# The opening product of each feature-major FFN up projection, made as two products of 128 tokens

## What is computed

```python
def swiglu(u, w1, w3, w2):
    return (jax.nn.silu(u @ w1) * (u @ w3)) @ w2

for i in range(DEPTH):                      # DEPTH = 2
    h = h + 0.5 * swiglu(rmsnorm(h, g_ffn1[i]), w1_ffn1[i], w3_ffn1[i], w2_ffn1[i])
    ...
    h = h + 0.5 * swiglu(rmsnorm(h, g_ffn2[i]), w1_ffn2[i], w3_ffn2[i], w2_ffn2[i])
    ...
```

## Time and profile before

| | us |
|---|---|
| median of three runs | 1600.23 |
| the profiled execution's own time | 1600.87 |
| its span, first to last instruction | 1599.1 |
| PE busy | 1556.6 (97%) |
| PE weight loads busy (they overlap PE) | 1457.3 (91%) |
| VectorE busy | 1077.4 (67%) |
| ScalarE busy | 805.8 (50%) |
| GpSimd busy | 149.7 (9%) |

### The profile page before, as it was taken

How to read it: one execution, slowest core, us unless ns; L and a number is a source line. 1 busy time by engine, 2 the same in 40 slices (tenths; PEclk the granted TensorE clock), 3 DMA queues, 4 the chain that set the end, 5 groups by cost and what they waited for, 6 DMA issues and landing times.

```text
span 1599.1 us, 28101 instructions
## 1 busy us (share of the span) xinstructions
PE 1556.6 (97%) x11554; PEld 1457.3 (91%) x11554; DVE 1077.4 (67%) x1309; ACT 805.8 (50%) x1133; POOL 149.7 (9%) x150
## 2 busy tenths in 40 slices
PE   7999999899999999999999999989999999999997
PEld 6999998899999979999899999979999999799996
DVE  5556578788787656555765556888787865555555
ACT  5444384665645345443564435745656534544344
POOL 1000003133130000000000000133132200000000
PEclk9999999999999999999999999999999999999999
DMA  7565543455545546655566555435554465466551
GB/s 245 190 197 189 175 142 110 132 156 149 168 132 184 205 160 195 197 186 192 163 192 193 192 187 159 133 106 159 168 147 131 158 206 195 145 212 193 187 184 66
DMA packets 245090, 271.09 MB, mean 170 GB/s; under 512 B 12561, under 2 KB 226153, under 8 KB 245013
## 3 DMA queue, kind: packets, MB, share of 16 engines
q1 hardware_dynamic: 239504, 266.90, 52.5%
q10 hardware_dynamic: 5364, 2.98, 0.7%
q0 software_dynamic: 144, 0.15, 0.0%
HBM read 268.94 MB, written 1.05 MB: 169 GB/s over the span
## 4 chain that ended last, share of the span: by engine, by line
PE 41%; issue 32%; DVE 17%; ACT 8%; POOL 1%; DMA 1%; ACTq 0%; DVEq 0%; SPq 0%; POOLq 0%
PE bank L1531 14%; PE bank L1454 11%; DVE w_lo L871 6%; PE bank L1484 4%; PE bank L1486 4%; PE bank L1485 4%; ACT w_hi L513 3%; DVE xcv L1111 2%; DVE zs L1162 1%; ACT R_lo L626 1%; DVE bcv L1111 1%; DVE xcv L1108 1%; PE bank L1878 1%; DVE xin L1097 1%; ACT R_hi L626 1%
## 5 line engine op out<-in xcount | busy, mean ns | idle before, releaser
L871 DVE TENSOR_TENSOR w_lo<-w_raw,w_hi 128x2048 fp32r<-128x2048 f32 x248 | 578.1, 2334 | 348.8 <-ACT w_hi L513 348.5
L513 ACT ACTIVATE w_hi<-w_raw 128x2048 fp32r<-128x2048 f32 x248 | 473.5, 1915 | 317.6 <-PE bank L1531 134.3
L1531 PE MATMUL bank<-f_hi,w_hi 128*128 128x256 f32 x1280 | 359.5, 281 | 0.0
L1531 PE MATMUL bank<-f_lo,w_hi 128*128 128x256 f32 x1280 | 359.2, 281 | 0.0
L1531 PE MATMUL bank<-f_hi,w_lo 128*128 128x256 f32 x1280 | 359.2, 281 | 0.0
L1454 PE MATMUL bank<-u_hi,w_hi 128*128 128x256 f32 x1152 | 328.1, 285 | 12.5 <-DVE w_lo L871 12.5
L1454 PE MATMUL bank<-u_lo,w_hi 128*128 128x256 f32 x1152 | 322.7, 280 | 0.0
L1454 PE MATMUL bank<-u_hi,w_lo 128*128 128x256 f32 x1152 | 322.6, 280 | 0.0
L1531 PEld LDWEIGHTS bank<-f_hi,w_lo 128*128 128x128 f32 x1280 | 245.3, 192 | 0.0
L1531 PEld LDWEIGHTS bank<-f_lo,w_hi 128*128 128x128 f32 x1280 | 240.3, 188 | 1.6
L1531 PEld LDWEIGHTS bank<-f_hi,w_hi 128*128 128x128 f32 x1280 | 240.3, 188 | 1.6
(11 more groups left out here) (294 smaller groups left out, 2417.8 us busy)
## 6 DMA issues: line engine op xcount, KB each, us to landing
w_raw<-in_w_ffn_dram SPq DMA_DIRECT2D x262, 512.0 KB, 4.4
w_raw<-in_w_in_dram SPq DMA_DIRECT2D x160, 512.0 KB, 4.9
w_raw<-in_w_branch_b_dram SPq DMA_DIRECT2D x32, 512.0 KB, 4.0
w_raw<-in_w_branch_a_dram SPq DMA_DIRECT2D x16, 512.0 KB, 4.3
w_raw<-in_w_out_dram SPq DMA_DIRECT2D x16, 512.0 KB, 4.0
w_raw<-in_w_ple_gate_dram SPq DMA_DIRECT2D x16, 512.0 KB, 4.5
y_feat<-in_w_ple_dram ACTq DMA_DIRECT2D x2, 1024.0 KB, 5.0
h<-in_x_dram SPq DMA_DIRECT2D x2, 512.0 KB, 5.5
```

Of the source, the lines that this page charges most:

```text
L513: a_.activation(whi[slot][:, :, :], raw[slot][:, :, :], ACT.Copy).then_inc(sem["w_hi"], 1)
L871: v_.tensor_tensor(wlo[slot][:, :, :], raw[slot][:, :, :], whi[slot][:, :, :].bitcast(F32), ALU.subtract).then_inc(sem["w_lo"], 1)
L1531: i = mm(o, four(w[slot])[:, k, cs], x[:, rows0 + k, :], start=(start and m % 2 == 0 and k + q == 0), stop=(not start and k == 3 and q == ...
```

## The change

In `up`, the very first product of a call with `start=True` (tile 0, model features 0 to 127, high by high) is made as two products, one for tokens 0 to 127 and one for tokens 128 to 255. Both have the same stationary operand. The first of them opens the bank, the second accumulates with `start=False`. The opening product of tile 2, in the other bank, stays whole, and so does all of the second call.

```diff
                         for k in range(4):
                             for q, (w, x) in enumerate(((whi, x2[0]), (whi, x2[1]), (wlo, x2[0]))):
-                                i = mm(o, four(w[slot])[:, k, cs], x[:, rows0 + k, :],
-                                       start=(start and m % 2 == 0 and k + q == 0),
+                                opens = start and m % 2 == 0 and k + q == 0
+                                if opens and m == 0:
+                                    mm(o[:, chunk(0)], four(w[slot])[:, k, cs], x[:, rows0 + k, chunk(0)],
+                                       start=True, stop=False, skip_group_check=True)
+                                    mm(o[:, chunk(1)], four(w[slot])[:, k, cs], x[:, rows0 + k, chunk(1)],
+                                       start=False, stop=False, skip_group_check=True)
+                                    continue
+                                i = mm(o, four(w[slot])[:, k, cs], x[:, rows0 + k, :], start=opens,
                                        stop=(not start and k == 3 and q == 2), skip_group_check=True)
```

## The result

The changed kernel takes **1588.78 us**, the median of four runs (1588.6 to 1590.43), against 1600.16 us before: a ratio of 0.9935 (95% interval 0.9923 to 0.9948), 0.65% faster. (The ratio is an estimate over all the runs; the two medians alone give 0.9929.) The forecast was 1604.8 us, with a range of 1600.3 to 1606.3. Its sign is wrong.

The account below looks back on a forecast made before the run. The prediction took TensorE's product stream in the FFN blocks as the bound. Two products at 116 ns for one of 118 gave +114 ns a block, 4.6 us over 40 blocks, hence 1604.8 us, range 1600.3 to 1606.3.

Parts of the forecast that it names:

- What bounds the kernel: In the FFN blocks everything follows TensorE; what a block's stream of products gains or loses, the kernel gains or loses.
- The price of the pair: At each block's opening product in `up`: two 128-column products at 116 ns replace one of 118, +114 ns a block.
- A slip in the working: Bounding the short product's price: four records with 40 moving columns, (0.64 - 0.28) / 3, were given as 119 ns a step.
- The sign to look for: From the last `down` product to the second 256-column product: distance grows from 0.23 + 0.12 us to about 0.46 us.
- 2 x 116 - 118: Two load-bound halves less the product they replace in each block: +114 ns, 4.6 us over 40 blocks.
- with everything else in them as before: In the changed profile 40 blocks lie 16.86 us apart instead of 16.75, their other contents unchanged.
- signs written down for being wrong: The argument fails if blocks stay at 16.75 us while the kernel slows, or PE shows a wait inside the blocks.
- The case "faster": Kernel gains only by a pair at 110 ns or shifted instruction fetching; the bound gives 0.3 us; chance 0.03.
- Rival A: Columns alone set the pair's price in each block, not slower: +10 ns a block, +0.4 us, 1600.6 us; chance 0.11.
- Rival B: Each short F32R half in `up` runs at the float32 rate, 224 ns: +13.2 us, 1613.4 us; chance 0.16.

Follow-up runs that it names:

- e3_both_calls: Against the kernel before: first product of tile 0 split into 128 and 128 tokens in both calls of `up`, not one; 1594.58 us, ratio 0.9962.
- e12_halves_earlier: Against the kernel before: `up` unsplit, the last but one 512-column product of each block's `down` made as two of 256; 1585.78 us, ratio 0.9912.

## Why the prediction was wrong

- **What bounds the kernel** was right. PE was the limit in the FFN blocks, and each block's change in length came through to the total: 36 x 0.294 us = 10.6 us against 10.4 us in the profiled time.
- **The price of the pair** was right. Forecast was +114 ns; the timeline gives 0.11 us, the second pair of e3_both_calls 0.13 us. The two splits that left the pace alone cost 0.13 us a block and made the kernel 4.9 and 5.2 us slower than the runs beside them, where 4.6 us was forecast. A slip in the working changes nothing: three steps in 0.64 - 0.28 = 0.36 us are 120 ns each, not 119. The sign to look for, a growth to "about 0.46 us", was set beside the recorded start of the first whole product, which came after 0.40 us with its duration stretched to 0.33; one product later the distance had grown by the 0.11 us that were meant.
- **The step that failed** is the sum "2 x 116 - 118", which held the other 94 products at 117.7 ns: "with everything else in them as before". They went to 113.3 ns, so a block gained 94 x 4.4 ns = 0.41 us that the sum didn't have, against the 0.11 us that it did. The 117.7 ns was taken as what a 256-column product costs, but it was one of two paces that the stream can have. The trace had both: medians of 281 ns beside minima of 276 ns, and a first call at 113 ns. The block length, from which the 117.7 ns was worked out, averages over a block and can't show that. None of the signs written down for being wrong was a block that gets shorter.
- **The range and the chances.** The case "faster" got 0.03 and a bound of 0.3 us, because only the new products' own price was bounded, not what they may do to the products behind them.
- **Rival A**, two products at 55 to 64 ns, was not what happened: the halves are 0.11 us apart in effect. The Trainium skill, "TensorE: Matmul & The Clock Gate", Back-to-back issue gap, has about 81 ns for 128 columns in a stream of load and product pairs. The runs don't bear that out for these float32 loads: a pair costs 0.11 to 0.13 us above one whole product, so 112 to 122 ns for each half. The same section gives N / 2.4 + 2.5 ns, 109 ns for 256 columns, as the gap of a product without a share for its load; both paces measured here lie above it. **Rival B** is refuted: each half is one record and no such price was paid.

**The cause, as far as it is shown.** A stream of load-and-product pairs with 256 columns runs at 113.3 or 117.7 ns in a product. It keeps its pace over the 48 to 96 products of one or two calls of `up` and into the next weight unit, and not always across small float32 products. It takes the pace from what stands at its entry or just ahead of it, within the first six products. Behind a wait the entry doesn't settle it: the mixer's run of 131 came out at either pace within one execution. That the kernel's gain is this pace, and not the pair's own price, is shown: splits of the same price that leave the pace alone are slower than the kernel before, and halving a product of `down` brings the pace without any pair. It is not the granted clock, which is 1.00 in the FFN blocks of both kernels, nor the values or the places of the operands behind the pair, which are the same in both kernels. The two FFNs of a layer keep the weights of `up` in different slots of the ring, and neighbouring blocks write different banks, and still all repeated blocks were slow before and fast after, 36 times out of 36. What was *not* settled is what inside TensorE differs between the two paces: recorded loads follow the start of a product by 3 to 4 ns in both. The slow pace shows as 5 ns more on each product and 4 ns more on the loads of low weights. Nor is it known which property of a split decides.

## What to carry to other kernels

In a dense stream of products, read the step between starts by stretches of equal products and compare medians with minima: two clusters a few per cent apart can mean that a pace is to be won for almost nothing. Then try small changes at the entry of the stream, and judge them by the steps behind, because the added product's own price says little. Here halving one product ahead of it shortened a block by 0.39 us; 96 products at 4.4 ns less are 0.42 us, which leaves about 0.03 us as the price, an estimate from these figures. And check first that PE limits the stage: the mixer's streams took the fast pace too, and its iterations stayed as long as they were.

## What was not expected of the hardware

- Two stable paces of the same F32R product at a granted clock of 1.00: 113.3 and 117.7 ns for 256 columns, and a third, 120 ns, with weights as the moving operand in halves.
- A stream can change from the slow to the fast pace at its fifth or sixth product, with nothing in the program at that place (e12_halves_earlier, 36 blocks alike).
- Splits of one product into 192 and 64 or into 64 and 192 columns, alike in price, that differ by 16 us in the kernel (1588.73 and 1604.76 us).
- A bf16 product of 32 columns in the stream costs 0.12 to 0.15 us: the product behind it starts 0.04 us later, and the one after that another 0.20 us in place of 0.12.
- Halving a 512-column product is free when it is done once (0.23 us either way), and costs 13 ns in 227 for each when all 24 are halved.
